# Four heads that begin with the scale alone, logits by feature quarter, spreading inside block 0

## The reference, cut to what matters

```python
sh1, sc1, g1, sh2, sc2, g2 = split(silu(c) @ w_ada + b_ada)      # one row per sequence, 9 rows
u   = x * (1 + sc1) + sh1                                        # 288 tokens x 2048
proj = u @ w_in        # hq, hf, hi, hg (HGRN2, 8 heads each), sq, sk, sv (stick-breaking, 8 heads each)
mix = concat(o_h, o_s) @ w_o                                     # after the recurrence and the attention
x   = layer_norm(ALPHA * x + g1 * mix, ln1_g, ln1_b)
u2  = x * (1 + sc2) + sh2
logits = u2 @ [w_gr | w_er] + bias                               # 4 groups, 32 experts; top 1 group, top 2 in it
y   = sum over the two experts of gate * (silu(u2 @ w_gate[e]) * (u2 @ w_up[e])) @ w_down[e]
x   = layer_norm(ALPHA * x + g2 * y, ln2_g, ln2_b)
```

## Time and profile before

| | before |
|---|---|
| median of 3 runs (lowest, highest) | 1757.49 us (1756.92, 1757.67) |
| profiled execution | 1752.23 us, its span 1750.5 us |
| PE busy | 1570.4 us, 90% of the span |
| DVE, ACT, POOL busy | 527.8, 200.1, 88.2 us |
| mean granted TensorE clock | 0.956 of full speed |
| DMA | 536.94 MB, mean 307 GB/s |
| chain that ended last | PE 68%, DMA 18%, DVE 5%, SP's queue 4% |

### The profile page before, as it was taken

The page is one execution under the profiler, slowest core; times in us unless marked ns, Lnnn a source line. Parts: engine busy times, 40 slices in busy tenths (PEclk is TensorE's granted clock), DMA queues, the critical chain, the costliest instruction groups (busy, mean ns, idle before and its releaser), DMA issues.

```text
span 1750.5 us, 24913 instructions
## 1 busy us (share of the span) xinstructions
PE 1570.4 (90%) x9577; PEld 891.4 (51%) x9577; DVE 527.8 (30%) x919; ACT 200.1 (11%) x335; POOL 88.2 (5%) x174
## 2 busy tenths in 40 slices
PE   3679999999999999899967999999989989889893
PEld 0036666633777765477735545454444434444351
DVE  0010008741221323432245232323223232232325
ACT  0000001200000012420025000000010000000002
POOL 4000000000010100010002000000000000000000
PEclk8679999999999999999986999999999999999997
DMA  9998888777343454364424999999999999999991
GB/s 357 422 395 321 327 310 326 309 302 288 133 162 98 167 199 148 132 241 165 141 99 169 399 411 417 403 425 424 415 402 418 418 396 416 407 425 417 417 388 61
DMA packets 79389, 536.94 MB, mean 307 GB/s; under 512 B 10385, under 2 KB 10561, under 8 KB 18065
## 3 DMA queue, kind: packets, MB, share of 16 engines
q1 hardware_dynamic: 72146, 507.62, 72.5%
q0 software_dynamic: 6576, 26.35, 4.5%
q10 hardware_dynamic: 624, 2.36, 0.3%
HBM read 533.40 MB, written 11.80 MB: 311 GB/s over the span
## 4 chain that ended last, share of the span: by engine, by line
PE 68%; DMA 18%; DVE 5%; SPq 4%; issue 2%; ACT 2%; ACTq 0%; DVEq 0%
PE ps L592 18%; DMA ring<-w_gate 14%; PE ps L1106 13%; PE ps L944 7%; PE ps L605 6%; PE ps L1126 6%; DMA ring<-w_ada 5%; PE ps L576 4%; SPq L384 3%; PE ps L1088 3%; PE ps L1052 1%; DVE arena L1928 1%; PE ps L796 1%; PE ps L610 1%; PE ps L1094 1%
## 5 line engine op out<-in xcount | busy, mean ns | idle before, releaser
L1106 PE MATMUL ps<-ring,arena 128*64 128x256 f32 x3200 | 359.2, 383 | 20.0 <-DMA ring<-w_gate 19.9
L592 PE MATMUL ps<-arena,ring 128*128 128x288 f32 x1280 | 322.2, 411 | 0.0
L1106 PEld LDWEIGHTS ps<-ring,arena 128*64 128x64 f32 x3200 | 227.5, 138 | 167.3 <-DMA ring<-w_gate 35.0
L592 PEld LDWEIGHTS ps<-arena,ring 128*128 128x128 f32 x1280 | 241.1, 191 | 89.6 <-issue 25.6
L1126 PE MATMUL ps<-arena 128*64 128x512 f32 x800 | 180.5, 597 | 23.5 <-DVE arena L1946 12.9
L576 PE MATMUL ps<-ring,silu_c 128*32 128x512 f32 x768 | 115.6, 711 | 53.4 <-DMA ring<-w_ada 26.5
L944 PE MATMUL ps<-arena,ring 128*128 128x288 f32 x512 | 124.7, 406 | 0.0
L1126 PEld LDWEIGHTS ps<-arena 128*64 128x64 f32 x800 | 54.0, 137 | 134.0 <-issue 90.7
L605 PE MATMUL ps<-ring,arena 128*128 128x512 f32 x256 | 115.2, 598 | 1.3 <-ACT arena L1190 0.7
L1088 PE MATMUL ps<-arena 64*128 64x512 f32 x384 | 104.6, 636 | 12.3 <-DVE arena L1928 10.7
L944 PEld LDWEIGHTS ps<-arena,ring 128*128 128x128 f32 x512 | 97.4, 190 | 26.6
(11 more groups left out here) (433 smaller groups left out, 1156.4 us busy)
## 6 DMA issues: line engine op xcount, KB each, us to landing
ring<-w_gate SPq DMA_DIRECT2D x100, 1024.0 KB, 24.1
ring<-w_up SPq DMA_DIRECT2D x100, 1024.0 KB, 26.1
arena<-w_down SPq DMA_DIRECT2D x100, 1024.0 KB, 26.6
ring<-w_ada SPq DMA_DIRECT2D x96, 1024.0 KB, 8.6
ring<-w_in SPq DMA_DIRECT2D x56, 1024.0 KB, 6.4
ring<-w_o SPq DMA_DIRECT2D x16, 1024.0 KB, 5.6
ring<-cache_k SPq DMA_DIRECT2D x16, 512.0 KB, 3.7
ring<-cache_v SPq DMA_DIRECT2D x16, 512.0 KB, 4.1
```

Of the source, the lines that this page charges most:

```text
L592: last = mm(ps[:, bank, 0:T], ring[:, slot, P * t:P * (t + 1)], uT[:, t, :], start=(t == 0), stop=(t == KC - 1))
L1106: last = mm(ps[B * s:B * (s + 1), 2 + c // 4, 0:256], xgT[:, 4 * (c % 4) + t, :], ring[:, c, 512 * t + 256 * s:512 * t + 256 * (s + 1)], s ...
```

## The change

1. The scale is made first, `uT` becomes x * (1 + sc1) by quarters, and four heads of the first head group are multiplied with that, between the chunks of the shift; their weights go to a buffer of their own, `w_first`. Then the shift is added to `uT`, its product with `w_first` is made by TensorE (16 products of 512 columns), turned, and added to the four heads. Heads 4 to 7 see the full `uT`, with four chunks of the next six ahead of each.
2. GpSimd waits for head 4 before it loads the first two states.
3. The sample part of `u2T` is made by quarters, and the logits wait quarter by quarter; `turn_tokens(0)` goes ahead of the turned logits.
4. ScalarE's table for Silu is loaded ahead of x1.
5. `xg` lies where the first tile's rows were; it is set to zero after that tile's store, and the gather no longer waits for the last transposes; the loads of `ln2` do.
6. All four `spread_columns` run in block 0, behind its gate and up chunks.

```diff
-        xg = area(4608, D, parts=B)
+        xg = area(16384, D, parts=B)
-        ln2s = area(16384, 2, 512)
-        xs = area(17408, 512)
+        ln2s = area(4608, 2, 512)
+        xs = area(5632, 512)
...
+        sh_order = [("ada", t) for t in range(5)] + [("head", 0)] + [("ada", t) for t in range(5, 10)] + [("head", 1)]
+        sh_order += [("ada", t) for t in range(10, KC)] + [("head", 2), ("head", 3)]
+        SH = {x: KC + i for i, x in enumerate(sh_order)}
+        SC2 = KC + len(sh_order)
...
+            for t in range(KC):
+                put(t + 1, t % SLOTS, w_ada[1, t])
+            for kind, i in sh_order:
+                n = SH[kind, i]
+                if kind == "ada":
+                    put(n + 1, n % SLOTS, w_ada[0, i])
+                else:
+                    sp.wait_ge(ring_used, n + 1)
+                    sp.dma_start(w_first[:, i, :], w_in[0, i]).then_inc(slot_loaded[n % SLOTS], 16)
+            for c in range(4, SLOTS):
+                for j in range(4):
+                    n = SC2 + 5 * (c - 4) + j
+                    put(n + 1, n % SLOTS, w_ada[2, 4 * (c - 4) + j])
+                n = SC2 + 5 * (c - 4) + 4
+                put(n + 1, n % SLOTS, w_in[0, c])
...
+            pool.wait_ge(ring_used, used(SC2 + 4))
             for h in range(2):
                 pool.dma_start(s0[h], state[:, h].rearrange("b p v -> p b v")).then_inc(s0_loaded[h], 16)
...
-                pool.dma_start(u2_rows[t0:t0 + tn, :], urow[i][0:tn, :]).then_inc(u2_stored, 16)
+                pool.dma_start(u2_rows[t0:t0 + tn, :], urow[i][0:tn, :]).then_inc(u2_stored if i else u2_first, 16)
+            pool.wait_ge(u2_first, 16)
+            link(g.memset(xg, 0.0))
...
-            pool.wait_ge(u2_act, KC)
-            pool.wait_ge(x1_act, KC)
-            pool.wait_ge(tt_pe, 24)
-            link(g.memset(xg, 0.0))
             pool.wait_ge(idx_made, 1)
             nc.gpsimd.tensor_copy(idx1[:], idxs[:, 0:1]).then_inc(idx_ready, 1)
             gather(1)
+            pool.wait_ge(tt_pe, 24)
             pool.dma_start(ln2b, ln2.partition_broadcast(P)).then_inc(late_loaded, 16)
...
+            for kind, i in sh_order:
+                n = SH[kind, i]
+                if kind == "ada":
+                    ada_chunk(n % SLOTS, loaded(n), i, 1)
+                    continue
+                pe.wait_ge(slot_loaded[n % SLOTS], loaded(n))
                 for t in range(KC):
+                    if i == 0 and t % 4 == 0:
+                        pe.wait_ge(u_ready, t // 4 + 1)
+                    last = mm(ps[:, 4 + i, 0:T], w_first[:, i, P * t:P * (t + 1)], uT[:, t, :],
+                              start=(t == 0), stop=(t == KC - 1))
+                last.then_inc(ring_used, 1)
+            ada_turn(2, 1)
+            for c in range(4, SLOTS):
+                for j in range(4):
+                    n = SC2 + 5 * (c - 4) + j
+                    ada_chunk(n % SLOTS, loaded(n), 4 * (c - 4) + j, 2)
+                if c == 4:
+                    pe.wait_ge(shp_ready, 1)
+                    for i in range(4):
+                        for j in range(4):
+                            t = 4 * i + j
+                            last = mm(ps[32 * j:32 * j + 32, 2, :].rearrange("p (h d) -> p h d", h=4), shp[:, t, :],
+                                      w_first[:, :, P * t:P * (t + 1)], start=(i == 0), stop=(i == 3))
+                    last.then_inc(fix_pe, 1)
...
+                if c == 4:
+                    pe.wait_ge(fix_dve, 1)
+                    for h in range(4):
+                        last = mm(ps[:, 3, 32 * h:32 * h + 32], fixp[:, P * h:P * (h + 1)], fold[:],
+                                  start=True, stop=True)
+                    last.then_inc(fix_pe, 1)
+            ada_turn(3, 2)
...
             for m in range(KC):
+                if m % 4 == 0:
+                    pe.wait_ge(u2_dve, m // 4 + 1)
                 pe.wait_ge(u2_act, m + 1)
-                if m == 0:
-                    pe.wait_ge(u2_dve, 1)
...
-            pe.wait_ge(tt_act, 20)
-            pe.wait_ge(xr_dve, 4)
-            pe.wait_ge(diag_ready, 1)
-            spread_columns((0, 1))
             pe.wait_ge(g2_act, 3)
             turn_rows(1)
-            pe.wait_ge(diag_ready, 2)
-            spread_columns((2, 3)).then_inc(where_pe, 1)
...
+                    with pe.If(i < 1):
+                        pe.wait_ge(tt_act, 20)
+                        pe.wait_ge(xr_dve, 4)
+                        pe.wait_ge(diag_ready, 2)
+                        spread_columns((0, 1, 2, 3)).then_inc(where_pe, 1)
                     turn_rows(i + 2)
...
+                if c == 4:
+                    act.wait_ge(ada_ready, 2)
+                    act.wait_ge(u_ready, 4)
+                    act.wait_ge(ring_used, used(SH["head", 3]))
+                    for q in range(4):
+                        for m in (4 * q + 2, 4 * q + 3):
+                            last = A(uT[:, m, 0:TP], uT[:, m, 0:TP], ACT.Identity, bias=adaT[:, 0, m, 0:1])
+                        last.then_inc(u_act, 1)
...
             A(m2, m2, ACT.Exp).then_inc(rt_act, 1)
-            act.wait_ge(u2_dve, 1)
+            nc.scalar.preload_act_table(ACT.Silu)
+            act.wait_ge(u2_dve, 4)
...
+            copy_rows_out(used(KC - 1), None)
+            add_bias(1, 1)
...
+            for q in range(4):
+                us = samp(uT[:, 4 * q:4 * q + 4, TP:T])
+                v.tensor_tensor(us, us, seq(adaT[:, 1, 4 * q:4 * q + 4, 1:R]), ALU.mult)
+                for m in range(4 * q, 4 * q + 4):
+                    last = v.tensor_scalar(uT[:, m, 0:TP], uT[:, m, 0:TP], adaT[:, 1, m, 0:1], None, ALU.mult)
+                last.then_inc(u_ready, 1)
+            first_head(1, SH["head", 1])
+            copy_rows_out(used(SH["ada", KC - 1]), 1)
+            first_head(3, SH["head", 3])
+            add_bias(0, 2)
+            dve.wait_ge(ada_ready, 2)
+            v.tensor_copy(shp[:, :, 0:R], adaT[:, 0]).then_inc(shp_ready, 1)
...
+            dve.wait_ge(fix_pe, 1)
+            v.tensor_copy(fixp, ps[:, 2, :]).then_inc(fix_dve, 1)
+            dve.wait_ge(fix_pe, 2)
+            link(v.tensor_copy(fixc, ps[:, 3, 0:P].rearrange("p (h r) -> p h r", h=4)))
...
+            for h in range(4):
+                v.tensor_scalar(hf[:, h, 0:TP], hf[:, h, 0:TP], fixc[:, h, 0:1], None, ALU.add)
...
+            def gain_sample(q):
+                ms = slice(4 * q, 4 * q + 4)
+                us = samp(u2T[:, ms, TP:T])
+                dve.wait_ge(ln_dve, q + 2)
+                link(v.tensor_tensor(us, samp(rT[:, ms, TP:T]), seq(adaT[:, 4, ms, 1:R]), ALU.mult))
+                v.tensor_tensor(us, us, seq(adaT[:, 3, ms, 1:R]), ALU.add).then_inc(u2_dve, 1)
             for q in range(1, 4):
                 centre(q)
                 scale_rows(q)
-            us, xs1 = samp(u2T[:, :, TP:T]), samp(rT[:, :, TP:T])
...
+                gain_sample(q - 1)
+            gain_sample(3)
```

More of the change, by code:

```diff
@@ L339, in _ @@
             sp.dma_start(pages[:], page_table[:]).then_inc(pages_loaded, 16)
[L340 to L343, removed]
+            for t in range(KC):
[13 more added lines that the diff above has]
+                put(n + 1, n % SLOTS, w_in[0, c])
+            with sp.Fori(1, 4) as g:
                 for c in range(SLOTS):
@@ L624, in _ @@
             pe.wait_ge(consts_ready, 1)
-            for six in range(2):
-                for t in range(KC):
[L627 to L633, removed]
+            for t in range(KC):
+                ada_chunk(t % SLOTS, loaded(t), t, None)
+            ada_turn(1, None)
+            for kind, i in sh_order:
[4 more added lines that the diff above has]
+                pe.wait_ge(slot_loaded[n % SLOTS], loaded(n))
+                for t in range(KC):
+                    if i == 0 and t % 4 == 0:
[3 more added lines that the diff above has]
+                last.then_inc(ring_used, 1)
@@ new lines, in _ @@
+            ada_turn(2, 1)
[11 more added lines that the diff above has]
+                    last.then_inc(fix_pe, 1)
+                n = SC2 + 5 * (c - 4) + 4
+                pe.wait_ge(slot_loaded[n % SLOTS], loaded(n))
+                pe.wait_ge((evac_act, evac_dve)[c % 2], 2 + c // 2 - 1)
+                for t in range(KC):
+                    if c == 4 and t % 4 == 0:
+                        pe.wait_ge(u_ready, 4 + t // 4 + 1)
+                        pe.wait_ge(u_act, t // 4 + 1)
+                    last = mm(ps[:, 4 + c % 4, 0:T], ring[:, n % SLOTS, P * t:P * (t + 1)], uT[:, t, :],
+                              start=(t == 0), stop=(t == KC - 1))
+                last.then_inc(ring_used, 1)
+                if c == 4:
[4 more added lines that the diff above has]
+                    last.then_inc(fix_pe, 1)
@@ L1018, in _ @@
             last.then_inc(rt_pe, 1)
-            for n in range(12):
+            for n in range(1, 12):
                 turn_tokens(n, u2T)
@@ new lines, in first_head @@
```

(22 more changed lines are left out.)

58 lines of the change are left out of this document (26 added, 32 removed).

## The result

| | before | after |
|---|---|---|
| median (lowest, highest; runs) | 1757.58 us (1756.92, 1760.48; 4) | 1729.54 us (1727.41, 1732.51; 4) |
| ratio, 95% interval | | 0.9839 [0.9818, 0.9860] |
| profiled execution, span | 1752.23, 1750.5 us | 1728.13, 1726.0 us |
| mean granted clock | 0.956 | 0.963 |

The kernel after is 28.0 us faster by medians; the interval makes that 24.6 to 32.0. The two profiled executions lie 24.5 apart by their spans. Line 600 is now `ada_chunk`'s product, 610 its turn, 662 heads 0 to 3, 676 the shift's product, 686 heads 4 to 7, 692 the fold (the four products that turn the shift's correction); 1060 the logits, 1075 `turn_tokens`, 1117 `turn_rows`, 1124 the spreading, 1165 the gate and up chunks, 1183 the turn of the hidden rows, 1190 the down product.

What follows compares the result with a forecast made beforehand. Arriving weight chunks bound the first stage and the experts, with TensorE heading the chain of waits between. 17.2 + 12.8 - 1 = 29 off the median 1757.5 gave 1728 us; own range 1722 to 1734, full range 1718 to 1741.

Steps and rivals of the forecast that it cites:

- term for starvation: Blocks 0 and 1: spreading in block 0 delays later weight releases; 1 us lost, bounds 0 to 5.
- first rival: Blocks 0 and 1: the weight stream starves, 5 to 8 us of the gain go, 1733 to 1736 us; chance 0.11.
- Part 1: Modulation and heads: heads 0 to 3 start with the scale alone; g1 turn at 172.0 instead of 189.22, gain 17.2 us.
- Stream: First stage: moving the two state loads behind head 4 brings the modulation chunks 2.9 us earlier; bounds nothing to 3.6.
- Head 2: Behind the shift chunks: its weights, the chunk after the last shift chunk, land at 102.9 us.
- slow start of 1.4: Heads 2 and 3: a slow-clock start adds 1.4 us to head 2's 7.96.
- rival of four slow heads: Heads 0 to 3: TensorE stays at the lower clock, 15.9 us per head, 5 us slower overall, 1762 us; chance 0.04.
- Part 2: Routing, logits to block 0: block 0 starts at 945.7 instead of 958.53, gain 12.8 us.
- lower bound: Logits: at half clock throughout they end at 915.7 instead of 916.6, 0.9 us earlier; 5.6 was taken.
- sign of being right: Expert stage: from block 0 to the last block it takes as long as now.
- stock: Expert stream at block 1: 5.6 us in hand, some 6.8 with the gather's half MB, so a delay of 5 fits.
- own sign of error: Expert stream: DMA share under 0.95 in the 40 us after block 0 would show the prediction wrong.

Runs made afterwards that it cites:

- states_early: Kernel after, without the wait that moves the state loads behind the five c4 chunks, so they start at the top again: 1732.17 us, ratio 0.9854.
- before again: Kernel before once more, unchanged, for its trace: span 1756.1 us, 705.5 us from the g1 turn to the sums.
- order_alone: Kernel before with only the new order of chunks and heads and the late state loads: 1737.90 us against 1758.42, ratio 0.9889.
- spread_before: Kernel after with the spreading back ahead of block 0, in two halves: 1729.42 us, ratio 0.9830.
- spread_mid: Kernel after with the spreading inside block 0, behind its fourth chunk: 1726.59 us, ratio 0.9827.
- with late table: Kernel after with the spreading in block 0's middle and the Silu table load back behind the copies of the gathered rows: 1719.06 us, ratio 0.9777.
- all_three: Kernel after with spreading in block 0's middle, late table load and the last layer norm's rows loaded earlier: 1722.54 us, ratio 0.9806.
- after again: Kernel after once more, unchanged, for its trace: 709.7 us from the g1 turn to the sums, 20.5 lost to half clock.
- routing_alone: Kernel before with only logits by quarter, early table load, earlier memset and spreading in block 0: 1749.81 us, ratio 0.9952.
- logits_whole: Kernel after, but TensorE begins the logits only once all four quarters of u2 stand: 1734.53 us, ratio 0.9868.
- table_late: Kernel after with only the Silu table load put back behind the copies of the gathered rows: 1726.46 us, ratio 0.9832.
- ln2_early: Kernel after with the 2 MB load of the last layer norm's rows issued once the u2 rows are stored: 1732.52 us, ratio 0.9857.

## Why the prediction was right

Forecast 1728, measured 1729.5. The mechanism held in both parts of the gain. The term for starvation was too small, and with it the first rival came true in its mechanism, at 4 to 5 us where it had 5 to 8. Part 1 was too small by nearly as much, so the two errors cancel: that the time came out within 1.5 us is partly luck.

**Part 1: 17.2 forecast, 20.1 in the trace, 20.5 by the medians of the half alone.** Between the means of the g1 turns (ten traces with the new order and late state loads, three with the old order) it is 19.5. Stream: 2.9 forecast, 58.57 to 55.61 in the traces, 2.64 back in `states_early`. Head 2 at 102.9 forecast, 102.67 measured: its weights were the new end. The largest excess is the slow start of 1.4 charged to heads 2 and 3: in the trace after there is none (15.79). It comes or not with the execution: five of the ten traces have 15.79, the other five 17.34 to 18.05, with turns from 168.8 to 171.3 in all. So 1.4 was a fair price, and the profiled execution a lucky one. Shift product 3.62 for 3.7, fold 0.97 for 0.8.

By the Trainium skill ("TensorE: Matmul & The Clock Gate", HAM oscillation — how this bites in real kernels) matmul groups shorter than the DMA wait between them start cold every time. The prediction took that to hold for the thin chunks; the traces agree only in part. Before, 6 of the 16 thin chunks from 60 to 101 us took 1.06 or 1.07 us, at full clock, some of them behind waits of 1.4 us; the others took 1.6 to 1.94. After, the last two thin chunks ahead of head 2, at 97.77 and 100.24, took 1.06 and 1.07 behind waits of 0.82 and 1.40, and head 1 took 8.03. The rival of four slow heads needed what the rows do not show: in the kernel after head 0 alone started slowly, and took 9.55 us.

**Part 2 up to block 0: 12.8 forecast, 13.1 measured.** Behind the sums, the logits end 6.4 us sooner (26.9 to 20.5) where I took 5.6. (My lower bound has a slip: 900.3 + 15.9 is 916.2 and not 915.7, which leaves 0.4 and not 0.9; the forecast does not use it.) The table load took 1.28 and left no gap: 903.55 + 0.19, 903.75, 905.05. The 1.38 us of drain that the Trainium skill ("ScalarE: Activation LUTs", What ACT_TABLE_LOAD costs) puts with every switch appears on neither side of it here. Yet the edit costs about 2.6 on the mean and not 1.28, because I priced an instruction on the path by its own duration, at a fixed clock: behind it the transposes ran longer at half clock in most traces. That 2.6 lies near the 2.66 us that the same section of the Trainium skill gives for load and drain together is chance, since x1 itself moves by 1.4.

**Starvation: 1 forecast, 4.0 between the two profiles, 4.9 between the means of the stages.** This is the step that was mis-sized, inside its bounds (0 to 5). The forecast's sign of being right, a stage as long as now, did not come. Stages by the place of the spreading:

| spreading | down product, us after block 0 | first `w_down` issue | stage |
|---|---|---|---|
| ahead (before, before again, `order_alone`, `spread_before`) | 17.0 to 18.5 | 19.0 to 20.5 | 791.0 to 792.0, mean 791.5 |
| middle (`spread_mid`, with late table, `all_three`) | 21.8 to 22.5 | 23.8 to 24.5 | 792.3 to 793.8, mean 793.1 |
| behind (after, after again, `routing_alone`, `states_early`, `logits_whole`, `table_late`, `ln2_early`) | 22.9 to 25.0 | 26.7 to 28.6 | 795.3 to 798.0, mean 796.4 |

Two errors lie in it. The delay was 6.7 us at the down product and not 5: I gave the plan read and the product 1 us, and VectorE idles 1.78 at the read and the loop's entry alone. And the stock was not 5.6: on the average SP's first `w_down` comes 8.2 us later for a stage 4.9 longer, and 4.4 later for one 1.6 longer, so about 3 us were in stock both times. This holds between the three groups; within the last, 26.7 us went with 796.0 and 28.1 with 795.3, so single traces scatter. The clock adds to it: behind its wait TensorE took 8.62 us for the down product where it took 7.09 before.

The prediction's own sign of error, a share under 0.95 in the 40 us after block 0, was badly chosen. The share there is 0.94 in the kernel after, but 0.92 in the kernel before, where the first 10 us have 0.65. The third 10 us of the kernel after, 0.81 in the rows on `ln2_early` above, differ from the same 10 us of the kernel before:

```profile
978.53:988.53 10.00, 9.63 (x56) 3.38 (x52) 3.28 (x5) 1.17 (x2) 0.18 (x1) 1.00 1.02 386
```

But `states_early` has 1.00 or more in each of its first four 10 us and still a stage of 796.05, so the share does not tell the stages apart. What does are the bytes of the first 100 us without the rows.

**The median.** The profiled execution of before lay 5.3 below its median; its loss of 10.2 us is the least of the 14 (with that of `states_early`), against 15.4 in the second trace of the same kernel. So subtracting the sum from the median was right, and the 4.7 us "lost" between the two profiles need no cause in the change: the second trace of the kernel before lost as much as the trace after. Without them the terms are 20.1 + 13.1 - 4.0 = 29.2, forecast 29, by medians 28.0.

## What to carry to other kernels

When work is moved off the path into the first round of a streamed loop, trace what it delays in that round: here, between the means of the groups, what the round's last release came later beyond about 3 us was paid nearly in full. Place such work where another engine's answer to it has TensorE work beside it, in the middle of a product and not at its end. Before a difference between two profiles is put down to the change, subtract TensorE's loss to half clock where TensorE leads (here it left 689.2 to 690.3 us in 14 traces), and take a second trace of each kernel.

## What the runs showed of the hardware

The half-clock stretches in the recurrence and the attention move from one execution of the same program to the next, and cost 10.2 to 20.5 us of some 700; `routing_alone` alone ran from 1740.07 us at a mean clock of 0.961 to 1754.60 at 0.952. I had not expected that a 1.28 us load on ScalarE goes with 2.6 us on the path, nearly half of them in stretches of TensorE at half clock, nor that taking 2 MB out of a full stream's first microseconds does not bring the end forward (stage 797.97 against 795.99).
